# Two spreads of a norm's root moved ahead, a wait for the ones matrix moved behind eight dense pieces

## What is computed

```python
h = h + rms_norm(f, norm_mlp_post)                 # end of the first block
hx = modulate(rms_norm_2(x, norm_g[i]), shift_x, scale_x)   # x is that h
hc = modulate(rms_norm_2(ctx, norm_g[i]), shift_c, scale_c)
qx, kx, vx, gx = split(hx @ w_in)                  # 8 heads, 2 maps of 64 each
qc, kc, vc, gc = split(hc @ w_in)
qx, kx = rope_axial(qx), rope_axial(kx)
s = q k^T * scale; p = softmax(s)                  # keys: context and latent
a = p[:, :, 0] - lam * p[:, :, 1]
o = rms_norm_2(a @ v, subln_g) * (1 - lam_init) * silu(g)
```

## Time and profile before

| | us |
| --- | --- |
| runs of the kernel before | 1640.92 median, 1640.31 to 1641.14, 3 runs |
| the profiled execution | 1641.54 |
| its span, first to last instruction | 1639.8 |
| mean granted TensorE clock, share of 2.4 GHz | 0.981 |
| PE busy, share of the span | 1555.7, 95% |

### The profile page before, as it was taken

The page is one execution under the profiler, slowest core; times in us unless marked ns, Lnnn a source line. Parts: engine busy times, 40 slices in busy tenths (PEclk is TensorE's granted clock), DMA queues, the critical chain, the costliest instruction groups (busy, mean ns, idle before and its releaser), DMA issues.

```text
span 1639.8 us, 23714 instructions
## 1 busy us (share of the span) xinstructions
PE 1555.7 (95%) x8392; PEld 1221.6 (75%) x8392; DVE 994.5 (61%) x2286; ACT 757.3 (46%) x1426; POOL 503.7 (31%) x231
## 2 busy tenths in 40 slices
PE   7998999999899999999969999999999989999998
PEld 5886666678688888888857877777777768876566
DVE  6235555355689767646666666675676267147854
ACT  6225766634342413233434544365445343248753
POOL 3651232244244444444211111121214343330012
PEclk9999999999899999999989999999999989999998
DMA  6861112264256565642211111111111112220001
GB/s 198 174 161 33 59 61 75 89 239 139 93 194 196 188 201 185 202 130 91 64 39 39 36 43 39 38 38 38 38 38 52 52 54 90 78 65 14 1 14 64
DMA packets 48401, 149.34 MB, mean 91 GB/s; under 512 B 5782, under 2 KB 9110, under 8 KB 48184
## 3 DMA queue, kind: packets, MB, share of 16 engines
q1 hardware_dynamic: 37080, 112.45, 22.8%
q10 hardware_dynamic: 11232, 35.72, 6.7%
HBM read 141.53 MB, written 6.62 MB: 90 GB/s over the span
## 4 chain that ended last, share of the span: by engine, by line
PE 80%; DVE 7%; ACT 6%; issue 5%; POOL 1%; DMA 0%; ACTq 0%; POOLq 0%; DVEq 0%
PE ps L357 41%; PE ps L361 20%; PE ps L582 4%; PE ps L593 3%; PE ps L563 3%; PE ps L1330 3%; PE ps L1370 3%; PE ps L1342 1%; PE ps L1089 1%; ACT sb L648 1%; ACT w_h L340 1%; PE ps L425 1%; DVE tg L1963 1%; DVE x2l L2036 1%; POOL w_l L985 1%
## 5 line engine op out<-in xcount | busy, mean ns | idle before, releaser
L985 POOL TENSOR_TENSOR w_l<-raw,w_h 128x1024 fp32r<-128x1024 f32 (+1 forms) x190 | 456.2, 2402 | 908.2 <-ACT w_h L340 888.6
L340 ACT ACTIVATE w_h<-raw 128x1024 fp32r<-128x1024 f32 x190 | 200.5, 1057 | 351.0 <-PE ps L357 292.8
L357 PE MATMUL ps<-x2h,w_h 128*128 128x512 f32 (+2 forms) x784 | 233.7, 363 | 34.0 <-DVE ones_r L2317 15.7
L357 PE MATMUL ps<-x1h,w_h 128*128 128x512 f32 x584 | 237.4, 407 | 16.6 <-POOL w_l L985 10.9
L357 PE MATMUL ps<-x1h,w_l 128*128 128x512 f32 x584 | 230.2, 394 | 0.0
L361 PE MATMUL ps<-x1l,w_h 128*128 128x512 f32 x584 | 229.6, 393 | 0.0
L361 PE MATMUL ps<-x2l,w_h 128*128 128x512 f32 (+2 forms) x784 | 220.8, 346 | 0.0
L357 PE MATMUL ps<-x2h,w_l 128*128 128x512 f32 (+2 forms) x784 | 220.3, 345 | 0.0
L357 PEld LDWEIGHTS ps<-x2h,w_h 128*128 128x128 f32 x784 | 126.4, 190 | 63.1 <-issue 19.0
L357 PEld LDWEIGHTS ps<-x1h,w_h 128*128 128x128 f32 x584 | 111.3, 191 | 40.9 <-POOL w_l L985 11.3
L357 PEld LDWEIGHTS ps<-x2h,w_l 128*128 128x128 f32 x784 | 126.6, 189 | 19.5
(11 more groups left out here) (344 smaller groups left out, 2694.7 us busy)
## 6 DMA issues: line engine op xcount, KB each, us to landing
raw<-in_w_mlp SPq DMA_DIRECT2D x64, 512.0 KB, 3.8
mraw<-in_w_mod ACTq DMA_DIRECT2D x51, 512.0 KB, 4.1
raw<-in_w_a SPq DMA_DIRECT2D x32, 512.0 KB, 3.6
raw<-in_w_att SPq DMA_DIRECT2D x25, 512.0 KB, 11.4
raw<-in_w_b SPq DMA_DIRECT2D x20, 512.0 KB, 3.6
raw<-in_w_g SPq DMA_DIRECT2D x16, 512.0 KB, 3.7
raw<-in_w_ao SPq DMA_DIRECT2D x9, 512.0 KB, 3.5
gates<-g_stage ACTq DMA_DIRECT2D x16, 256.0 KB, 2.2
```

The source lines that it names most:

```text
L340: nc.scalar.activation(split(u)[0], raw[:, u % RAW], ACT.Copy).then_inc(w_hi, 1)
L357: mm = nc.tensor.matmul(o, w[:, k], xh(k), start=(first and k == k0 and wi == 0), stop=(last and k == k1 - 1 and wi == 1))
L985: nc.gpsimd.tensor_tensor(l[:, ks], raw[:, u % RAW, ks], h[:, ks].bitcast(F32), ALU.subtract).then_inc(w_lo, 1)
```

## The change

Four edits, all in the passage to the first heads.

1. PE spreads the root directly behind the eight tiles of the first two units, ahead of unit 2, not in its middle, and twice: into bank 7 as before and into bank 6. ACT copies `rstd` from bank 6 once both are there; `modulated` on DVE starts when the first is. `first_ctx(3)`, which writes bank 6, waits for ACT's copy.
2. DVE starts with the first two `x_tile`s and puts the evictions of q and k behind them. ACT shifts those two tiles ahead of `take_first` of q and k.
3. PE's wait for `ones_r` moves from ahead of all heads into head 0, behind its first dense pieces and the wait for the gate, ahead of `scores(0)`.
4. Eight dense pieces stand ahead of `scores(0)`, where there were nine; the piece left over and those behind it shift back, until the count is level again from `turns(3)` on.

```diff
@@ norms @@
-        nm3b = Norm(add=0, mm=0)
+        nm3b = Norm(add=0, mm=0, r=2)
@@ PE, units of head 0 @@
-            first_x(2, 4, 0, 4)
             nm3b.wait(pe, "rc", 1)
             spread(7, 0, 4).then_inc(nm3b.r, 1)
-            first_x(2, 4, 4, KT)
+            spread(6, 0, 4).then_inc(nm3b.r, 1)
+            first_x(2, 4, 0, KT)
             nm3b.wait(pe, "src", KT)
             first_ctx(2, 5, 0, KT).then_inc(unit, 1)
+            pe.wait_ge(n3_r, 1)
             first_ctx(3, 6, 0, KT)
@@ PE, attend @@
                 if lead:
-                    dense(9)
+                    dense(8)
                     wait_head(pe, "g", head, 1, 1)
+                    pe.wait_ge(ha["ones"], 1)
...
                 for qt in range(4):
                     scores(qt + 2)
-                    dense(1 if lead else 2 if more else 4 + (qt == 0))
+                    dense(1 + (qt > 2) if lead else 2 if more else 4 + (qt == 0))
                     turns(qt)
-                    dense(1 + qt // 2 if lead else 1 + qt % 2 if more else 3)
+                    dense(1 + (qt > 1) if lead else 1 + qt % 2 if more else 3)
...
-            pe.wait_ge(ha["ones"], 1)
             all_heads(pe, attend)
@@ ACT @@
-            nm3b.wait(act, "r", 1)
-            nc.scalar.activation(rstd[:, 0:S], ps[:, 7], ACT.Copy).then_inc(n3_r, 1)
+            nm3b.wait(act, "r", 2)
+            nc.scalar.activation(rstd[:, 0:S], ps[:, 6], ACT.Copy).then_inc(n3_r, 1)
...
-            take_first(0, a_q, -0.125).then_inc(ha["q"], 1)
-            take_first(1, a_k, 1.0).then_inc(ha["k"], 1)
             for k in range(KT):
                 nm3b.wait(act, "t", k + 1)
                 shift_tile(k, 0, xn2, 0).then_inc(nm3b.hi, 1)
+                if k == 1:
+                    take_first(0, a_q, -0.125).then_inc(ha["q"], 1)
+                    take_first(1, a_k, 1.0).then_inc(ha["k"], 1)
@@ DVE @@
-            def modulated(nm, l, buf, ws):
+            def modulated(nm, l, buf, ws, begun=None):
...
                     ins.then_inc(nm.t, 1)
+                    if k == 1 and begun:
+                        begun()
...
+            def evict_pair():
+
+                v.wait_ge(n3_r, 1)
+                evict_first(0, 0, 1, -0.125)
+                evict_first(1, 2, 3, 1.0)
             invert(v, nm3b, S)
-            v.wait_ge(n3_r, 1)
-            evict_first(0, 0, 1, -0.125)
-            evict_first(1, 2, 3, 1.0)
-            modulated(nm3b, 0, xn2, (0,))
+            modulated(nm3b, 0, xn2, (0,), evict_pair)
```

## The result

| | before | after |
| --- | --- | --- |
| median, runs | 1641.03 us (1640.31 to 1641.91, 4) | 1626.86 us (1625.28 to 1629.44, 4) |
| profiled execution, its span | 1641.54, 1639.8 | 1625.28, 1623.2 |
| mean granted clock of the profiled execution | 0.981 | 0.988 |

The changed kernel takes 0.9919 of the time before, interval 0.9904 to 0.9934; the medians differ by 14.2 us. In a second set of runs it took 1628.81 (1626.41 to 1634.13, 6 runs) beside 1640.33, ratio 0.9932, interval 0.9916 to 0.9948; the medians differ by 11.5 us. The forecast was 1629.0 and 11.9 less.

What follows compares the result with a forecast made beforehand. PE's order bounds it: dense pieces wait 15.7 us for `ones_r`, which only the scores need. First scores 11.9 us earlier (851.5 against 863.40) and head 0 unchanged take the median 1640.92 to 1629.0; range 1626.6 to 1633.0.

Steps and rivals of the forecast that it cites:

- PE's units and pieces: PE ahead of the first scores: head 0's units end at 836.2, eight dense pieces follow at once, up to 844.6.
- DVE to the gate: DVE ready for the gate's line at 836, PE's unit starts it at 836.4; the chain gains 1.3 us.
- The hold in the rotation of k: POOL's work, released earlier, newly holds DVE's rotation of head 0's k: 1.7 us, bounds 0 and 2.2.
- Sum to the first scores: Head 0's first scores on PE start at 851.5 against 863.40, 11.9 us earlier.
- Head 0: Head 0's length, 45.85 us before: terms +1.05, +1.6, -1.2 and -1.7 sum to -0.25, rounded to 0.
- the dip between 880 and 890: Half-speed clock in head 0, 3.4 us long, goes as the wait for head 1's k shrinks: -1.7 us.
- The slow clock at the start: Head 0's first work runs at 1.2 GHz behind PE's idle stretch: +1.6 us, bounds 0.8 and 3.3.
- The wait for k: PE's wait in head 0 for head 1's k, 2.32 us before, shrinks: -1.2 us.
- No new hold: Rival: POOL's work misses the rotation of k, scores(0) at 849.8, gain 13.6, time 1627.3; chance 0.13.
- Head 0 paced by DVE and ACT: Rival: head 0 keeps its wait for k and slow clock, 1631.7, or lasts 52.4, 1635.5; chance 0.12.
- The clock stays low: Rival: half-speed clock persists through head 0 behind the 6.9 us idle, costing 20 to 40 us, about 1650; chance 0.03.
- Nothing moves: Rival: another wait, such as the tiles, holds the dense pieces at 836 and the gap stays, 1640.9; chance 0.02.

Runs made afterwards that it cites:

- one-spread kernel: Changed kernel without the second spread (into bank 6); ACT copies bank 7 and DVE waits for that copy ahead of its tiles: 1625.68 us, ratio 0.9913.
- late split: Changed kernel with ACT's split of head 1's v unit moved behind head 0's first two exponentials: 1626.83 us, ratio 0.9922.
- nine pieces: Changed kernel with nine dense pieces ahead of the first scores and the earlier distribution of the rest: 1629.09 us, ratio 0.9935.
- fourteen pieces: Changed kernel with 14 dense pieces ahead of the first scores in place of 8, and ACT taking head 1's k early: 1621.19 us, repeated 1623.11.
- fourteen, old norm: Changed kernel with 14 dense pieces ahead of the first scores, head 1's k taken early, and edits 1 and 2 undone: 1624.26 us, ratio 0.9899.
- the kernel with one spread besides: Changed kernel with 14 dense pieces ahead, the split of head 1's v unit behind head 0's first exponentials, and one spread instead of two: 1620.77 us.

## Why the prediction was right, point by point

**What bounds it** was right: the gap went with the order on PE, and edits 3 and 4 alone show it.

**PE's units and pieces.** Head 0's units end with one spread more: the first piece was put at 836.2, which is R + 19.5 in the trace of before; it starts at R + 19.41 (two spreads take 1.70 us, 814.30 to 816.00, where one was put at 0.81). Eight pieces end at about R + 27.8. Right. The tiles were there; no piece waited.

**DVE to the gate.** Line 2193 (now 2199) was put at 836.4, R + 19.7, with PE's last unit as what starts it. It starts at R + 19.88, but PE's last unit is not what starts it: DVE comes to it without a wait, and PE's last matmul, begun at 832.50 with 0.39 us, was through 0.2 before DVE took the unit up at 833.13. DVE was carried through to 836, R + 19.3, which was 0.5 early; that PE's 836.2 came so near was luck. What paces DVE there is a PE unit all the same, the third, through ACT's split and POOL's hold of the fifth `low_tile`, as the rows of the one-spread kernel show (0.9 earlier all along). The prediction had both steps, the hold and ACT's wait for the third unit, but not that they set the line. The chain gained 1.1, not 1.3.

**The hold in the rotation of k**, the step with the widest bounds (0 to 2.2, taken 1.7): 1.95, shown by the late split. POOL began at 843.20 and DVE's line 2215 at 843.44, so POOL was first and DVE waited it out. The Trainium skill, "SBUF — State Buffer", section "Who interferes with whom", has the first to be issued keep the port; the trace agrees (POOL took its 2.34 us, DVE 2.64 us where free it takes 0.69), but the case I weighed, in which line 2209 goes first and free, did not come about.

**Sum to the first scores.** 851.5 was said, in the time of the trace before; R + 35.31 is 852.04 there. 0.5 late: 0.2 of it the chain, 0.25 the hold, the rest instructions of the chain and the step from `ones_r` to PE. 11.4 us instead of 11.9.

**Head 0** was put at no change; it was 0.44 longer in one profile and 0.03 shorter in the other. The sum came out near by cancelling. Of its terms the piece (+1.05) stands and the dip between 880 and 890 is gone (-1.7, right in size; that the shorter wait for k removed it is not shown, since with nine pieces the wait of 2.33 was back and no dip followed). The slow clock at the start was put at +1.6 and was mis-sized; it measured up to +3.0:

```profile
844.60:848.60 4.00, 0.00 (x0) 0.00 (x0) 3.83 (x5) 0.00 (x0) 0.94 (x1) 0.50 0.43 124
848.63:854.60 5.97, 5.96 (x26) 4.92 (x28) 1.84 (x6) 2.09 (x5) 0.00 (x0) 0.50 0.01 4
854.80:860.00 5.20, 5.20 (x39) 4.13 (x38) 4.00 (x12) 2.42 (x5) 0.00 (x0) 1.00 0.00 0
```

PE had been idle since 841.3. The clock is at 0.50, 1.2 GHz, through the last 4 us of the pause and for another 6 us of head 0's work, up to 854.7, which costs half of that, 3.0. The wait for k was put at -1.2 and measured -1.9 (2.32 to 0.43). 1.05 + 3.0 - 1.9 - 1.7 = 0.45, and head 0 measured +0.44. The same sum holds for the others: what of head 0's work falls in the slow stretch varies with the run and the kernel, 5.1 us in the second profile, 4.0 with edits 3 and 4 alone (3.7 at 0.50 and a little of the stretch behind it, which has 0.98). The second profile:

```profile
849.30:854.40 5.10, 5.10 (x22) 4.39 (x23) 1.85 (x6) 1.80 (x4) 0.00 (x0) 0.50 0.01 4
```

Edits 3 and 4 alone:

```profile
851.67:855.40 3.73, 3.73 (x17) 3.12 (x18) 1.43 (x5) 0.43 (x1) 0.00 (x0) 0.50 0.00 0
855.50:860.00 4.50, 4.50 (x33) 3.68 (x31) 2.32 (x10) 3.15 (x8) 0.00 (x0) 0.98 0.00 0
```

Head 0 shortens with it, 46.29, 45.82, 45.29: half a us for each us. The other kernels with eight pieces fit: 5.5 us and 46.20 with one spread, some 3.7 and 45.21 with the late split. This also says why edits 1 and 2 bring next to nothing beside edits 3 and 4: they end the pause 1.0 us earlier, and head 0 then begins 1.0 us deeper in the slow stretch. The longer pause had hidden more of it. This is read from the profiles, one or two of each kernel; where the slow stretch ends differs by up to a us between the two of the changed kernel. In the changed kernel's second profile half of that us was kept, in the first nothing.

**Rivals.** *No new hold* is refuted (2.64 against 0.69), although the median of the first set, 1626.86, lies nearer to its 1627.3 than to the forecast's 1629.0. *Head 0 paced by DVE and ACT* is refuted at eight pieces, and at fourteen too: 38.71 us, with no wait of PE over 1.05. *The clock stays low* did not happen; it was at 0.50 for 10 us in all, 4 of them in the pause. *Nothing moves* did not happen.

**What was not foreseen** is the part of the medians that this place doesn't hold: 14.2 in the first set against 10.9 to 11.4 in the place. It lies in unchanged code at another mean clock, and the second set, 11.5, has none of it. The forecast's own sum fits the place to 0.5 to 1.0 us.

## What to carry to other kernels

When one engine's long wait has an operand that its next work doesn't read, move the wait down to the first reader and pull independent work up into the pause, as many pieces as the pause is long; then look at who else that early work wakes, since here it started a POOL pass inside the DVE chain that everybody waited for (2.0 us). Take fillers from a later place only with the eviction or copy that they wait for moved along, or the pause comes back there. Count edits worth under 3 us from an anchor just ahead of the change to one just behind it, since the clock in unchanged code moves the total by as much, and read the clock in that stretch too: 1.55 of the 2.6 us between the old and new norm with fourteen pieces were clock.

## What the runs showed of the hardware

- The mean granted clock of one program varies from run to run (0.982 to 0.988 for the changed kernel), and the time goes with it, loosely: 3.4 us from 0.983 to 0.988, more than most single edits here, but a run at 0.940 (fourteen pieces) was only 2.2 above the median of its set. A pause of PE of 7 us cost up to 3.0 us beyond itself, in work at 0.50 behind it; pauses of 1.05 and 0.99 us cost nothing (PEclk 1.00 in all of its stretches with fourteen pieces), one of 1.91 was followed by a stretch of 0.83 and one of 2.99 (fourteen, old norm) by one at 0.50, while one of 2.33 (nine pieces, 869.48) and one of 1.93 (the kernel with one spread besides) were not.
- How much work ran at 0.50 behind a pause did not follow the pause's length: 4.0 us behind 9.29, 5.1 to 6.0 behind 7.37, some 3.7 behind 5.40, 5.0 behind 5.05 (nine pieces). So a pause that ended 1.0 us sooner gave nothing or half a us, and one that ended 3.0 us sooner (the late split) all of it.
- A DVE instruction held by POOL ends about 0.55 us behind POOL's end in all four cases of the changed kernel, and is then through. Free, these instructions take 0.69 to 0.75; held, they took 1.31 to 2.87, by how long POOL's pass still ran. Whether a longer one would end as soon behind POOL no run shows.
